# x's first block loaded in two halves over two DMA queues, and idle products moved between its turns

## The chip, the cores and the metric

The kernel runs on one core of a Trainium2 chip. The time is the device time of one execution in microseconds (us); runs of one kernel mostly agree within 0.3%. The engines are TensorE (PE; its weight loads are listed apart as PEld), VectorE (DVE), ScalarE (ACT), GpSimd (POOL) and SyncE (SP), which here only issues DMAs. ScalarE and GpSimd can issue DMAs as well.

## The reference, cut to what matters

One block of a hybrid of attention and mLSTM over 512 tokens of width 1024, float32:

```
h = rms_norm(x, pre_norm_g)                       # x: 512 x 1024
proj = einsum('bsd,dc->bsc', h, w_in)             # 1024 x 4616
aq, ak, av, az, mq, mk, mv, mo, mz, mi, mf = split_columns(proj)
ya = rms_norm(moba_attention(rope(aq), rope(ak), av), attn_out_g) * silu(az)
ym = sigmoid(mo) * norm(mlstm(silu(conv(mq, mk)), mv, mi, mf)) * mlstm_out_g * silu(mz)
x + rms_norm(concat(ya, ym) @ w_out, post_norm_g)
```

Only the very start matters here: x times the columns of w_in that give mv.

## The kernel before, in words

Every large product is made of three products of float32r parts: high by high, high by low, low by high, where a high part is a rounded copy and a low part what is left. x must lie with its features on the partitions, so TensorE turns it first: x is loaded in blocks of 128 features (`X_CHUNKS`, `load_x`, L558 to L561), one block is four tiles of 128 tokens by 128 features, and four products with the identity turn them into a bank of PSUM. ScalarE then copies the bank as the high part (`x_hi`; for block 0 in two halves of 256 tokens, `x_hi_half`, L827 to L831), times the pre-norm weights, and VectorE makes the low part (`x_low`, `x_low_half`, L1124). The norm's factor for each token comes in later.

w_in is cut into slots of 128 rows by 512 columns. SP loads them in order, between the blocks of x: block 0, slot 0, block 1, slot 1 and so on. VectorE rounds slots 0 and 1 (L1128, L1133), ScalarE the later ones (L824), and VectorE makes the low part of each (`cut`, L1101).

The order of work around the change is written out by hand, engine by engine, and each engine runs its own list in order. TensorE's list begins so: six idle products of 512 columns (`keep_busy(6)`, L1568), a turn of the 8 x 128 pre-norm weights (L1574, waits for the identity and their load `par_in`), the turn of tiles 0 and 1 of block 0 and then of tiles 2 and 3 (`turn_x_half(0)` and `turn_x_half(1)`, L1579), four idle products of 256 columns, and then the real products of slot 0 (`mv_slot(0)`, L1606): tiles 0 and 1, tiles 2 and 3 with x's high part, the same with its low part, the turn of block 1 (`turn_x(1)`, L1586), and the four products with the slot's low part. Idle products multiply ones by ones into a bank that is not read. ScalarE's list begins with the load of the pre-norm weights (L853), a small activation that brings its table in (L854), and the two halves of block 0 (L830). `x_squares` (L839) sums the squares of x much later.

Of the kernel before, what the change touches and what calls it, by code (L numbers as in the profile page):

```python
# [23 lines left out]
P = 128  # L24
SEQ = 512
D = 1024
NT = SEQ // P
NK = D // P
AW = 512
# [41 lines left out]
HALF_SEQ = SEQ // 2  # L71
# [10 lines left out]
def width(n):  # L82

    return MZ_W if S_MZ <= n < S_MZ + NK else AW
# [149 lines left out]
def unit(u):  # L234

    return NT - 1 - u // AH, u % AH
# [27 lines left out]
def build(nc, x, pre_g, w_in, i_bias, f_bias, conv_w, conv_b, attn_g, mlstm_g, w_out, post_g, rope, out):  # L264
    with ExitStack() as ctx:
# [3 lines left out]
        def sem(name):  # L269
            return ctx.enter_context(nc.semaphore(name))  # L270
# [54 lines left out]
        def f_part(at, *shape):  # L325
            n = int(np.prod(shape))
            v = farena[:, at:at + n]
            return v if len(shape) == 1 else v.rearrange("p (a b) -> p a b", a=shape[0]) if len(shape) == 2 \
                else v.rearrange("p (a b c) -> p a b c", a=shape[0], b=shape[1])
# [7 lines left out]
        x_sb = f_part(F_X, NT, D)  # L337
# [11 lines left out]
        rows = [gy[0:16, i // 4, i % 4, :] for i in range(8)]  # L349
# [53 lines left out]


        x_in = [sem(f"x_in{c}") for c in range(len(X_CHUNKS))]
        par_in = sem("par_in")
        rope_in = sem("rope_in")
        post_in = sem("post_in")
# [125 lines left out]
        def low_done(eng, n):  # L534

            eng.wait_ge(w_lo_done[n % 2], n // 2 + 1)
# [4 lines left out]
        def turn_tile(n):  # L541

            _, kind, i = TURNS[n]
            return 0 if kind == "ym" else 4, NT - 1 - i


        def store(sp, i):
            t = NT - 1 - i
            for c in range(2):
                cols = slice(c * AW, (c + 1) * AW)  # L550
                sp.wait_ge(out_ready, 2 * i + c + 1)
                sp.dma_start(out[0, t * P:(t + 1) * P, cols], xr[i][:, cols]).then_inc(out_done[i], 16)

        @block.sync
        def _(sp):
            x2 = x.rearrange("b s d -> (b s) d")

            def load_x(c):  # L558
                k, n = X_CHUNKS[c]
                cols = slice(k * P, (k + n) * P)  # L560
                sp.dma_start(x_sb[:, :, cols], x2[:, cols].rearrange("(t p) d -> p t d", p=P)).then_inc(x_in[c], 16)  # L561

            def rows_out(w, m):

                sp.wait_ge(kq_ready, NT * w + m + 1)
                sp.dma_start(kq_dram[w, :, ROT * m:ROT * m + ROT, :], by_dims[:, m, :]).then_inc(kq_out[w], 16)

            def rows_back(w, m):

                sp.wait_ge(kq_out[w], 16 * NT)  # L570
                if w:
                    sp.wait_ge(kt_lo, NT)
                sp.dma_start(whole[:, m, :], kq_dram[w, 2 * m:2 * m + 2].rearrange("h d s -> (h d) s"))\
                    .then_inc(kq_moved[w], 16)

            for n, (mat, kind, k, c) in enumerate(SLOTS):
                if n in X_BEFORE:
                    load_x(X_BEFORE[n])
                if n >= RAW:
                    low_done(sp, n - RAW)  # L580
                w = w_in if mat == "in" else w_out
                if kind == "cols":
                    src = w[0, k * P:(k + 1) * P, c:c + width(n)]
                    dst = w_raw[:, n % RAW, 0:width(n)]
                else:
                    src = w[0, k * P:(k + 4) * P, c:c + MD].rearrange("(k p) c -> p k c", p=P)
                    dst = w_raw[:, n % RAW, :].rearrange("p (k c) -> p k c", k=4)
                sp.dma_start(dst, src).then_inc(raw_in[n % RAW], 16)
                if n == S_QK + 6:
                    sp.wait_ge(ssx_done, NT)  # L590
                    sp.dma_start(gains[:], attn_g.to_broadcast([P, AW])).then_inc(gain_in, 16)
                for w in range(2):
                    for c in range(2):
                        if n == OUT_AT[w] + c:
                            rows_out(w, 2 * c)
                            rows_out(w, 2 * c + 1)
                        if n == BACK_AT[w] + c:
                            rows_back(w, 2 * c)
                            rows_back(w, 2 * c + 1)
                if n == S_AQ + 4:  # L600
                    sp.wait_ge(az_gained, NT)
                    sp.dma_start(gains[:], mlstm_g.to_broadcast([P, AW])).then_inc(gain_in, 16)
            sp.wait_ge(v_lo_done, NT)
            sp.dma_start(post, post_g.to_broadcast([P, D])).then_inc(post_in, 16)

            def load_residual(i):
                t = NT - 1 - i
                sp.dma_start(xr[i], x2[t * P:(t + 1) * P, :]).then_inc(xr_in[i], 16)

            sp.wait_ge(ym_gated, NT)  # L610
            load_residual(0)
            load_residual(1)
            sp.wait_ge(turn_ps, TURN_OF["ym", NT - 1] + 1)
            load_residual(2)
            load_residual(3)
            store(sp, 0)
            store(sp, 1)
            store(sp, 2)
            sp.wait_ge(out_ready, 2 * NT - 1)
            sp.dma_start(out[0, 0:P, 0:AW], xr[NT - 1][:, 0:AW]).then_inc(out_done[NT - 1], 16)  # L620
            sp.wait_ge(out_ready, 2 * NT + 1)
            sp.dma_start(out[0, 0:P, quarter[1]], xr[NT - 1][:, quarter[1]]).then_inc(out_done[NT - 1], 16)
            for i in range(NT):
                sp.wait_ge(out_done[i], 32 + 16 * (i == NT - 1))
# [188 lines left out]
        def _(a):  # L813
# [12 lines left out]
            def x_hi_half(q):  # L826
                half = slice(q * HALF_SEQ, (q + 1) * HALF_SEQ)  # L827
                a.wait_ge(xt_ps, q + 1)
                a.wait_ge(par_done, 1)
                a.activation(xT_hi[:, 0, half], bank[4 + q][:, half], ACT.Copy, scale=pcol[:, R_PRE:R_PRE + 1])\  # L830
                    .then_inc(xt_hi, 1)  # L831
# [7 lines left out]
            def x_squares(t):  # L839
                if t:  # L840
                    a.wait_ge(ssx_done, t)
                for c in range(len(X_CHUNKS)):
                    a.wait_ge(x_in[c], 16)
                a.activation(silu_az[:, 0:2, :].rearrange("p a c -> p (a c)"), x_sb[:, t, :], ACT.Square, accum_out=ssx[:, t:t + 1]).then_inc(ssx_done, 1)
# [6 lines left out]
                             scale=rx[:, t:t + 1]).then_inc(mv_hi_done, 1)  # L851

            a.dma_start(prow[:], pre_g.rearrange("o (c p) -> (o c) p", p=P)).then_inc(par_in, 16)  # L853
            a.activation(ssx[:, 0:1], ones, ACT.Copy)  # L854
            x_hi_half(0)
            x_hi_half(1)
# [2 lines left out]
            for k in range(1, NK):  # L859
                if k > 1:  # L860
                    cut(k)
                    x_hi(k)
                if k >= 5:
                    x_squares(k - 5)
            cut(RING)
            x_squares(NT - 1)
            for n in range(RING + 1, RING + 6):
                cut(n)
# [160 lines left out]
            for s in range(STEPS):  # L1029
# [18 lines left out]
                for kind, what in events:  # L1048
# [7 lines left out]
                    elif kind == "y_sq":  # L1056
                        i, c = what
# [6 lines left out]
                    elif kind == "y_q_sq":  # L1064
                        q = what[0]
# [484 lines left out]
        def _(pe):  # L1550
# [14 lines left out]
            def keep_busy(n, cols=AW):  # L1565

                for _ in range(n):
                    pe.matmul(bank[7][:, 0:cols], ones.to_broadcast([P, P]), ones.to_broadcast([P, cols]), start=True,  # L1568
                              stop=True)
# [4 lines left out]
            pe.transpose(bank[6][:, 0:R_AG], prow[:], ident[0:R_AG, 0:R_AG]).then_inc(par_ps, 1)  # L1574

            def turn_x_half(q):
                pe.wait_ge(x_in[0], 16)
                for t in (2 * q, 2 * q + 1):
                    mm = pe.transpose(bank[4 + q][:, t * P:(t + 1) * P], x_sb[:, t, 0:P], ident[:])  # L1579
                mm.then_inc(xt_ps, 1)  # L1580
# [129 lines left out]


            turn_x_half(0)
            turn_x_half(1)
            keep_busy(4, AW // 2)
            for k in range(NK - 1):
                mv_slot(k)
            mix_slot(0)
# [78 lines left out]
            def turn(n):  # L1796

                _, kind, i = TURNS[n]
                t = NT - 1 - i
                pe.wait_ge(ym_gated if kind == "ym" else ya_gated, i + 1)  # L1800
                if turn_bank(n) == TURN_BANK:
                    pe.wait_ge(masked, min(TURNS[n][0], NU))
                else:
                    pe.wait_ge(ya_summed, (TURNS[n][0] - LAG_YT) // 4 + 1)
                src = ym[:, t] if kind == "ym" else silu_az[:, t]
                for k in range(4):
                    mm = pe.transpose(bank[turn_bank(n)][:, k * P:(k + 1) * P], src[:, k * P:(k + 1) * P], ident[:])  # L1807
                mm.then_inc(turn_ps, 1)
# [90 lines left out]
            for s in range(STEPS):  # L1899
# [16 lines left out]
                if 0 <= u < NU:  # L1916
                    t, h = unit(u)
# [56 lines left out]
```

## Time and profile before

| | us |
|---|---|
| median of 3 runs | 313.82 (313.65 to 314.89) |
| the profiled execution | 313.44 |
| its span, first to last instruction | 311.7 |
| TensorE busy | 305.2 (98%) |
| VectorE, ScalarE, GpSimd busy | 227.4, 164.7, 92.5 |

The profile is of one execution, and its times start with its span. The span is what the engines' instructions cover; the execution's time is 1.74 us more. The busy time of TensorE counts products whose ends are modelled, so it says that TensorE always has work, not how well it is used. The mean granted clock is 0.995.

### The profile page before, as it was taken

The page shows a single profiled execution, that of the slowest core. Times are in us where ns is not written, and L with a number is a line of the kernel's source. Part 1 is how long each engine was busy: PE and PEld are TensorE (multiplying, and loading weights), DVE is VectorE, ACT ScalarE, POOL GpSimd, SP SyncE. Part 2 cuts the span into 40 slices and gives each one's busy share as a digit, 9 for nine tenths or more (in the row PEclk, how much of TensorE's full clock was granted, in tenths as well). Part 3 has the DMA queues.
Part 4 walks back from the last instruction along what each step waited for, and adds up shares of the span by engine and source line. Part 5 has one row for each costly group of instructions (what it writes and reads, how often), then busy time and mean ns, then how long its engine had stood idle before and what let it go on. Part 6 is the DMA issues. An engine that isn't in the chain of part 4 may idle for free.

```text
span 311.7 us, 5015 instructions
## 1 busy us (share of the span) xinstructions
PE 305.2 (98%) x1609; PEld 257.2 (83%) x1609; DVE 227.4 (73%) x511; ACT 164.7 (53%) x338; POOL 92.5 (30%) x110
## 2 busy tenths in 40 slices
PE   8999999999999999999999999999999999999992
PEld 5788888888888888888888899887888888888892
DVE  3544899957999499967999447997676867766534
ACT  3467684578337324384244583494746867452301
POOL 1711005174340004000040017538922984000000
PEclk9999999999999999999999999999999999999997
DMA  7933463565423545752554432410110463310111
GB/s 214 336 79 91 116 196 98 161 199 139 151 67 94 162 142 164 236 167 73 151 173 170 133 103 67 127 63 19 67 67 2 137 219 131 125 67 0 69 67 68
DMA packets 28953, 38.28 MB, mean 123 GB/s; under 512 B 2552, under 2 KB 16236, under 8 KB 28928
## 3 DMA queue, kind: packets, MB, share of 16 engines
q1 hardware_dynamic: 27440, 34.51, 36.7%
q0 software_dynamic: 1328, 3.32, 3.1%
q8 instruction: 13, 0.21, 0.3%
q10 hardware_dynamic: 160, 0.14, 0.1%
q14 instruction: 12, 0.10, 0.1%
HBM read 33.68 MB, written 4.28 MB: 122 GB/s over the span
## 4 chain that ended last, share of the span: by engine, by line
PE 94%; issue 3%; DVE 0%; DVEq 0%; ACT 0%; POOLq 0%; POOL 0%; ACTq 0%
PE bank L1553 25%; PE bank L1555 24%; PE bank L1554 24%; PE bank L1606 4%; PE bank L1924 3%; PE bank L1859 3%; PE bank L1883 3%; PE bank L1701 2%; PE bank L1807 1%; PE bank L1568 1%; PE bank L1586 1%; PE bank L1873 1%; PE bank L1702 1%; PE bank L1895 0%; PE bank L1579 0%
## 5 line engine op out<-in xcount | busy, mean ns | idle before, releaser
L824 ACT ACTIVATE w_hi<-w_raw 128x512 fp32r<-128x512 f32 (+1 forms) x72 | 43.6, 616 | 60.6 <-PE bank L1555 49.4
L1553 PE MATMUL bank<-w_hi,xT_hi 128*128 128x512 f32 (+2 forms) x180 | 71.0, 395 | 0.0
L1555 PE MATMUL bank<-w_hi,xT_lo 128*128 128x512 f32 (+2 forms) x180 | 68.0, 378 | 0.0
L1554 PE MATMUL bank<-w_lo,xT_hi 128*128 128x512 f32 (+2 forms) x180 | 67.7, 376 | 0.0
L1553 PE MATMUL bank<-xT_hi,w_hi 128*128 128x512 f32 x136 | 54.0, 397 | 0.0
L1555 PE MATMUL bank<-xT_hi,w_lo 128*128 128x512 f32 x136 | 53.3, 392 | 0.0
L1554 PE MATMUL bank<-xT_lo,w_hi 128*128 128x512 f32 x136 | 53.1, 390 | 0.0
L1101 DVE TENSOR_TENSOR w_lo<-w_raw,w_hi 128x512 fp32r<-128x512 f32 (+1 forms) x66 | 45.9, 705 | 8.6 <-ACT w_hi L824 8.4
L1555 PEld LDWEIGHTS bank<-w_hi,xT_lo 128*128 128x128 f32 x180 | 33.8, 188 | 5.8
L1553 PEld LDWEIGHTS bank<-w_hi,xT_hi 128*128 128x128 f32 x180 | 33.9, 188 | 5.0 <-issue 0.4
L1554 PEld LDWEIGHTS bank<-w_lo,xT_hi 128*128 128x128 f32 x180 | 34.0, 189 | 4.5
L1555 PEld LDWEIGHTS bank<-xT_hi,w_lo 128*128 128x128 f32 x136 | 25.5, 188 | 5.6
L1554 PEld LDWEIGHTS bank<-xT_lo,w_hi 128*128 128x128 f32 x136 | 25.6, 188 | 4.7
L1553 PEld LDWEIGHTS bank<-xT_hi,w_hi 128*128 128x128 f32 x136 | 25.6, 188 | 4.7
L1027 ACT ACTIVATE rarena<-bank 128x512 fp32r<-128x512 f32 (+3 forms) x32 | 14.0, 437 | 20.8 <-PE bank L1924 20.8
L1419 DVE CUSTOM_DVE_ANT_0 farena<-bank,causal 128x512 f32<-128x512 f32 (+3 forms) x32 | 15.3, 482 | 8.6 <-PE bank L1859 8.2
L1425 DVE TENSOR_TENSOR rarena<-bank,rarena 128x512 fp32r<-128x512 f32 (+3 forms) x32 | 15.6, 486 | 7.8 <-ACT rarena L1027 7.4
L1231 DVE SCALAR_TENSOR_TENSOR farena<-bank,farena 128x512 f32<-128x512 f32 (+3 forms) x16 | 7.8, 490 | 16.4 <-PE bank L1555 16.4
L1019 ACT ACTIVATE farena<-farena,mx 128x512 f32<-128x512 f32 (+3 forms) x32 | 17.9, 560 | 3.4 <-DVE mx L1419 3.3
L1211 DVE SCALAR_TENSOR_TENSOR farena<-farena,pcol 128x512 f32<-128x512 f32 x24 | 18.8, 782 | 0.9
L669 POOL TENSOR_TENSOR vr<-vs,mhalf 128x2 f32<-128x2 f32 x8 | 5.7, 711 | 44.0 <-DVE vs L1270 44.0
L1924 PE MATMUL bank<-ident,farena 128*128 128x128 f32 x80 | 14.6, 280 | 0.0
(214 smaller groups left out, 571.0 us busy)
## 6 DMA issues: line engine op xcount, KB each, us to landing
w_raw<-in_w_in SPq DMA_DIRECT2D x66, 256.0 KB, 2.9
w_raw<-in_w_out SPq DMA_DIRECT2D x16, 256.0 KB, 2.6
farena<-g_rows POOLq DMA_DIRECT2D x4, 640.0 KB, 3.9
kq_rows<-stage SPq DMA_DIRECT2D x8, 256.0 KB
gy<-kq_rows SPq DMA_DIRECT2D x8, 256.0 KB, 3.5
gy<-in_x SPq DMA_DIRECT2D x4, 512.0 KB, 5.2
out_y<-gy SPq DMA_DIRECT2D x7, 256.0 KB, 2.1
w_raw<-in_w_in SPq DMA_DIRECT2D x8, 196.0 KB, 3.4
```

The lines of the kernel that those rows point to most:

```text
L824: a.activation(hi, raw, ACT.Copy).then_inc(w_hi_done, 1)
L1019: a.activation(prob[:, s % 2, 0:n], sm[:, s % 2, 0:n], ACT.Exp, scale=-1.0, bias=mx[:, s:s + 1], accum_out=rsum[:, s:s + 1]).then_inc(prob ...
L1027: a.activation(pT[:, 2 * (u % 2), 0:n], bank[4 + u % 2][:, 0:n], ACT.Copy).then_inc(pt_hi, 1)
L1101: v.tensor_tensor(lo, raw, hi, ALU.subtract).then_inc(w_lo_done[n % 2], 1)
L1211: ins = v.scalar_tensor_tensor(out=acc, in0=u[:, j:j + SEQ], scalar=tap[j], in1=acc, op0=ALU.mult, op1=ALU.add)
L1419: v.tensor_tensor_reduce(sm[:, s % 2, 0:n], bank[score_bank(s)][:, at:at + n], causal[:, SEQ - n:], -Q_SCALE, BIG, ALU.add, ALU.min, mx[:, ...
L1425: v.tensor_tensor(pT[:, 2 * (u % 2) + 1, 0:n], bank[4 + u % 2][:, 0:n], f32(pT[:, 2 * (u % 2), 0:n]), ALU.subtract).then_inc(pt_lo, 1)
L1553: pe.matmul(o, hi, m_hi, start=start, stop=False)
L1554: pe.matmul(o, hi, m_lo, start=False, stop=False)
L1555: return pe.matmul(o, lo, m_hi, start=False, stop=stop)
L1606: mm = pe.matmul(bank[t][:], xs[:, k, t * P:(t + 1) * P], ws, start=k + term == 0, stop=False)
L1924: mm = pe.transpose(bank[4 + u % 2][:, j * P:(j + 1) * P], prob[:, u % 2, j * P:(j + 1) * P], ident[:])
```

## The change

Block 0 of x is loaded by two DMAs in place of one: tokens 0 to 255 by SP as before, at the same place, and tokens 256 to 511 by ScalarE, behind the load of the pre-norm weights, with a semaphore of its own, `x_rest_in`. The turn of tiles 2 and 3 waits for that semaphore in place of `x_in[0]`, and the squares wait for both. Of the four idle products of 256 columns behind the turns, two go between the two halves of the turn.

```
+        x_rest_in = sem("x_rest_in")
...
             def load_x(c):
                 k, n = X_CHUNKS[c]
                 cols = slice(k * P, (k + n) * P)
-                sp.dma_start(x_sb[:, :, cols], x2[:, cols].rearrange("(t p) d -> p t d", p=P)).then_inc(x_in[c], 16)
+                rows = slice(0, SEQ if c else HALF_SEQ)
+                sp.dma_start(x_sb[:, 0:NT if c else NT // 2, cols], x2[rows, cols].rearrange("(t p) d -> p t d", p=P))\
+                    .then_inc(x_in[c], 16)
...
             def x_squares(t):
                 if t:
                     a.wait_ge(ssx_done, t)
+                a.wait_ge(x_rest_in, 16)
...
             a.dma_start(prow[:], pre_g.rearrange("o (c p) -> (o c) p", p=P)).then_inc(par_in, 16)
+            a.dma_start(x_sb[:, NT // 2:NT, 0:P], x.rearrange("b s d -> (b s) d")[HALF_SEQ:SEQ, 0:P]
+                        .rearrange("(t p) d -> p t d", p=P)).then_inc(x_rest_in, 16)
...
             def turn_x_half(q):
-                pe.wait_ge(x_in[0], 16)
+                pe.wait_ge((x_in[0], x_rest_in)[q], 16)
...
             turn_x_half(0)
+            keep_busy(2, AW // 2)
             turn_x_half(1)
-            keep_busy(4, AW // 2)
+            keep_busy(2, AW // 2)
```

## Rows read from the trace of the kernel before

**Rows 1.** The page: busy time with shares, and the last chain by engine.
```profile
PE 305.2 (98%) x1609; PEld 257.2 (83%) x1609; DVE 227.4 (73%) x511; ACT 164.7 (53%) x338; POOL 92.5 (30%) x110
...
PE 94%; issue 3%; DVE 0%; DVEq 0%; ACT 0%; POOLq 0%; POOL 0%; ACTq 0%
```

**Rows 2.** The chain of waits from 0 to 8 us: start, us, what.
```profile
0.85 2.72 PE bank L1568 x6
3.56 0.20 PE bank L1574
3.77 1.04 PE bank L1579 x4
4.81 0.45 PE bank L1568 x4
5.26 1.85 PE bank L1606 x8
```

**Rows 3.** Timeline of TensorE's weight loads, in narrow windows: start, us, what, count.
```profile
3.49 0.18 PEld L1574 LDWEIGHTS bank<-ident,prow 8*128 8x128 f32 x1 [0.84 <-issue]
...
3.69 0.18 PEld L1579 LDWEIGHTS bank<-ident,farena 128*128 128x128 f32 x1
...
3.69 0.29 PEld L1579 LDWEIGHTS bank<-ident,farena 128*128 128x128 f32 x2
...
4.39 0.15 PEld L1568 LDWEIGHTS bank<-const-bfloat16-1.0 128*128 128x128 bf16 x1
...
5.01 0.19 PEld L1606 LDWEIGHTS bank<-w_hi,xT_hi 128*128 128x128 f32 x1
...
5.37 0.19 PEld L1606 LDWEIGHTS bank<-w_hi,xT_hi 128*128 128x128 f32 x1
```

**Rows 4.** Timeline of DMA issues; landings of block 0, slot 0, all x.
```profile
0.81 0.45 SPq L561 DMA_DIRECT2D farena<-in_x  x1
0.81 0.60 ACTq L853 DMA_DIRECT2D prow<-in_pre_norm_g  x1
...
1.32 0.48 SPq L588 DMA_DIRECT2D w_raw<-in_w_in  x1
...
DMA to landing us min/median/max: 2.8/2.8/2.8
...
DMA to landing us min/median/max: 2.9/2.9/2.9
...
DMA to landing us min/median/max: 2.8/5.2/6.8
```

**Rows 5.** Turns of block 0 and of block 1: ns min/median/max, first and last start.
```profile
L1579 PE MATMUL bank<-ident,farena x4: 421/421/474, 3.7 to 4.4; 128*128 128x128 f32 x4
...
L1586 PE MATMUL bank<-ident,farena x4: 270/272/272, 7.0 to 7.3; 128*128 128x128 f32 x4
```

**Rows 6.** Windows: us, busy of PE, PEld, DVE, ACT, POOL, clock, DMA share, GB/s.
```profile
2.00:3.00 1.00, 1.00 (x4) 0.29 (x2) 0.00 (x0) 0.94 (x2) 0.00 (x0) 1.00 0.98 271
...
5.40:9.00 3.60, 3.60 (x19) 2.77 (x18) 2.84 (x6) 1.12 (x2) 0.00 (x0) 1.00 1.02 332
```

**Rows 7.** Timeline of ScalarE and VectorE.
```profile
1.46 1.28 ACT L854 ACT_TABLE_LOAD   x1 [1.46 <-PEq L1966]
...
4.37 0.43 DVE L1128 CAST w_hi<-w_raw 128x512 fp32r<-128x512 f32 x1 [0.40 <-DMA w_raw<-in_w_in]
...
4.42 0.90 ACT L830 ACTIVATE xT_hi<-bank,pcol 128x256 fp32r<-128x256 f32 x2 [1.47 <-PE bank L1579]
...
5.76 0.68 DVE L1101 TENSOR_TENSOR w_lo<-w_raw,w_hi 128x512 fp32r<-128x512 f32 x1
```

**Rows 8.** Timeline of TensorE's products, in narrow windows.
```profile
4.39 0.42 PE L1579 MATMUL bank<-ident,farena 128*128 128x128 f32 x1
...
4.60 0.44 PE L1568 MATMUL bank<-const-bfloat16-1.0 128*128 128x256 bf16 x2
...
5.04 0.70 PE L1606 MATMUL bank<-w_hi,xT_hi 128*128 128x512 f32 x2
```

More of the change, by code:

```diff
@@ L405, in build @@
         x_in = [sem(f"x_in{c}") for c in range(len(X_CHUNKS))]
+        x_rest_in = sem("x_rest_in")
         par_in = sem("par_in")
@@ L560, in load_x @@
                 cols = slice(k * P, (k + n) * P)
-                sp.dma_start(x_sb[:, :, cols], x2[:, cols].rearrange("(t p) d -> p t d", p=P)).then_inc(x_in[c], 16)
+                rows = slice(0, SEQ if c else HALF_SEQ)
+                sp.dma_start(x_sb[:, 0:NT if c else NT // 2, cols], x2[rows, cols].rearrange("(t p) d -> p t d", p=P))\
+                    .then_inc(x_in[c], 16)
             def rows_out(w, m):
@@ L841, in x_squares @@
                     a.wait_ge(ssx_done, t)
+                a.wait_ge(x_rest_in, 16)
                 for c in range(len(X_CHUNKS)):
@@ L853, in _ @@
             a.dma_start(prow[:], pre_g.rearrange("o (c p) -> (o c) p", p=P)).then_inc(par_in, 16)
+            a.dma_start(x_sb[:, NT // 2:NT, 0:P], x.rearrange("b s d -> (b s) d")[HALF_SEQ:SEQ, 0:P]
+                        .rearrange("(t p) d -> p t d", p=P)).then_inc(x_rest_in, 16)
             a.activation(ssx[:, 0:1], ones, ACT.Copy)
@@ L1576, in turn_x_half @@
             def turn_x_half(q):
-                pe.wait_ge(x_in[0], 16)
+                pe.wait_ge((x_in[0], x_rest_in)[q], 16)
                 for t in (2 * q, 2 * q + 1):
@@ L1712, in _ @@
             turn_x_half(0)
+            keep_busy(2, AW // 2)
             turn_x_half(1)
-            keep_busy(4, AW // 2)
+            keep_busy(2, AW // 2)
             for k in range(NK - 1):
```

## The prediction

> **What bounds the kernel now.** I began with the busy row and the engine shares of the chain that ended last [rows 1]. TensorE is busy for 305.2 of 311.7 us and it is 94% of the chain, so the end moves only if TensorE does more or less, or meets a hole. The change touches nothing behind the first weight slot. The profile as a whole is therefore not what decides. What decides is whether the first six microseconds of TensorE have a hole that the change closes, or get one that it opens.
>
> So I read the chain in order of time next, for the first 8 us [rows 2]. It never leaves TensorE. Six idle products run from 0.85, then the product that turns the pre-norm weights, then the four products that turn x's first block, then four idle ones, and real products from 5.26. No DMA and no other engine stands in it. A reader who hopes that an earlier x brings an earlier start must find the wait for x first, and this view shows none.
>
> A chain can hide a short wait, because ends of products are modelled. So I took the timeline of TensorE's weight loads next, which are where its waits sit [rows 3]. The load for the pre-norm product starts at 3.49, and the first load that needs x at 3.69. Between the first and the second load for turning x there is 0.07 us only (3.69 and 3.76: the row of two lasts 0.29, the row of one 0.18, and the second load begins before the first has ended). So a load that waits for nothing may follow so fast. x's block was issued at 0.81 and landed 2.8 us later, at 3.6 [rows 4]. The landing may thus hold back the first turn by up to 3.69 - (3.49 + 0.07) = 0.13 us. By the chain, which gives the pre-norm product the time until 3.77, it holds back nothing. This is all that an earlier first half can win.
>
> The durations also show in which clock this happens. The turning products of x's first block take 421 ns in the median and start over 0.7 us (3.7 to 4.4), those of the second block take 270 to 272 ns and start over 0.3 (7.0 to 7.3), of the same form [rows 5]. By this, the engine is at the lower of its two levels (1.2 GHz) for the turns and at 2.4 GHz in the idle products after them: four of them take 0.45 us of the chain, 0.11 each for 256 columns, while the six before took 0.45 each for 512. The granted clock column says 1.00 from the start, so here durations have to be read and not the column. The rise lies at about 4.7.
>
> **The change part by part.**
>
> *First half on SP's queue.* The load keeps its issue, one instruction of 0.45 us [rows 4], and moves half the bytes. In the microsecond from 2 to 3 the DMA engines are 0.98 busy and move 271 GB/s [rows 6]. 131 KB fewer at this rate is 0.48 us, so the first half lands at about 3.1 in place of 3.6. TensorE's pre-norm product is still in front, at 3.49. The gain at the first turn is between 0 and 0.13 us (above). I take the middle, 0.07. This stretch lies ahead of the clock's rise: what is brought forward there is work at half the rate, and if the rise stays where it is, 0.07 us earlier at 1.2 GHz saves 0.03 us behind the rise.
>
> *The issue on ScalarE's queue.* One more DMA issue, 0.60 us by the one in front of it [rows 4]. Behind it on ScalarE are the table load (1.46, for 1.28 us) and an activation of one column [rows 7]; the table load ends 0.60 later, at 3.34. The next instruction of weight waits until 4.42, so 1.08 us of cover are left, less the small activation, and the cost is 0. Without that cover it would be 0.60. SP's issues keep their number and order.
>
> *The second half's landing, a new wait.* It is issued at 0.81 + 0.60 = 1.41. The first turn of the second half will be the fifth load of TensorE after the pre-norm one, the place that the first idle load has now: 4.39 [rows 3]. Behind this wait in TensorE's queue is everything. From below, it lands as fast as the unloaded rows do, 2.8 and 2.9 us after issue [rows 4]: 4.2 to 4.3, a margin of 0.1 to 0.2 us. It can't be below that in a way that gains, since nothing asks for it before 4.39. From above, the loads on SP's queue take up to 6.8 us to land, median 5.2, but behind up to a megabyte of their own queue [rows 4]. This would be 6.6 to 8.2, a hole of 2.2 to 3.8 us. The nearest rows are the two that were issued in the same first microsecond with little ahead of them, so I take 4.25 and no hole, and keep the rest for the range.
>
> *The first weight slot.* It is issued at 1.32, lands at 4.2 [rows 4], is rounded by VectorE from 4.37 for 0.43 us, to 4.80 [rows 7], and its first reader loads at 5.01 [rows 3]. The sum of x's block and the slot, 512 KB, is the same as before, only the order in which it is served changes. If the second half goes first everywhere the slot lands where it does today; if not, earlier. Neither costs: 0.2 us are in hand.
>
> The Trainium skill speaks against the change here. DMA: Bandwidth & Descriptors, section "Issuing engines are not separate DMA queues", says that transfers started by different engines run on the same 16 DMA engines and interleave, and that issuing from several saves only sequencer time. By that rule the second half brings no bandwidth and only takes turns with the slot; the trace agrees so far that the DMA engines stand at 0.98 and 1.02 busy from 2 to 3 and from 5.4 to 9 us with one queue [rows 6]. The sum by the rule is the same as mine, and a second queue with bandwidth of its own wouldn't lower it either, as TensorE isn't free to use an earlier landing.
>
> *Idle products two and two.* Their number stays four. Two of them move ahead of the rise, and two turns move behind it. A turn takes 0.21 us at the lower level (the three loads from 3.76 to 4.39) and 0.1 at the upper [rows 5]; an idle product of 256 columns takes 0.11 at the upper level (0.45 for four), and 0.22 at the lower, half of one of the six of 512 columns that take 2.72 together [rows 2, 3]. The trade is even, so TensorE's own time stays and the edit costs 0 by itself.
>
> What it does cost is order. ScalarE rounds the two halves of x's first block one after the other, 0.90 us for both from 4.42 [rows 7]. It starts the second at about 4.85, when the fourth turn ends (4.39 + 0.42 = 4.81 [rows 8]). After the change the fourth turn takes the place of the second idle product. That one starts at about 4.77 (the row of two from 4.60 lasts 0.44 and ends at 5.04, and a product at the upper level with 128 columns lasts 0.27 [rows 5, 8]), so the turn ends at 5.04, ScalarE starts 0.04 later at 5.08 and ends at 5.55 with its half of 0.90 and a little. The third real product is the first that reads the second half of x. Its load comes 0.05 after ScalarE's end today (4.85 + 0.47 = 5.32, and 5.37 [rows 3]), so it comes at 5.60. After a load that had to wait, real products go on about 0.1 us later (the load at 5.01 had such a start: the row of two products from 5.04 lasts 0.70, the second of them 0.39 of it, so that one starts at 5.35; at 0.23 a product, 1.85 for eight, the first had its effective start at 5.12 [rows 2, 8]), thus 5.71 in place of the 5.58 where the third product stands now (5.35 + 0.23). This is a hole of 0.13 us, which I take. From below it is 0, if the turn keeps its end at 4.81; from above 0.35, if the two idle products ahead run wholly at the lower level and the turn ends 0.2 later. With the 0.03 of the earlier start it comes to 0.10.
>
> *What follows.* VectorE's two small parts of x start as late as ScalarE's second half, +0.23, so its cut of the first slot starts at 5.99 for 0.68 and ends at 6.67. It is read behind the turn of block 1, whose last product starts at 7.3 [rows 5, 7]: 0.6 us of cover. The sums of squares wait for the new semaphore too, but they wait for all blocks of x already, and the last of these is issued long behind the second half: 0. Everything after that is TensorE's own queue, moved as one block.
>
> **Sum.** 313.44 us for the profiled execution (311.70 span, 1.74 around it), -0.03 + 0.13 = 313.54. The median of the runs is 313.82, 0.38 above the profiled execution; with the same 0.10 it is 313.92, so I say 313.9.
>
> **The rivals.**
>
> *The second half comes too late (slower).* It is on the queue that was issued at 1.41 and takes turns with the slot's packets of 2 KB, with its own of 512 bytes. Place: TensorE's wait ahead of the third turn. It decides from a landing after 4.39. Each 0.1 us is 0.1 us of hole, partly at the lower level. For it: only 0.1 to 0.2 us of margin, engines 0.98 busy. Against it: few bytes ahead of it in its queue (4 KB), and both rows of the first microsecond landed within 2.9. Price: landing at 4.9 gives 0.5 us, 314.4; the far bound of 3.8 gives 317.7.
>
> *The clock rises later (slower).* TensorE has been fed without a hole for 3.9 us from 0.85 when it rises. If a hole ahead of 4.7 puts the rise off, each us at 1.2 GHz loses half a us of work. To be slower by 0.5%, 1.57 us, it would have to come 3.1 us later. For it: one new wait exactly there. Against it: no hole expected, or a short one. Price, for as much again as the first 3.9 us: 1.95 us, 315.8. TensorE: Matmul & The Clock Gate, "The HAM clock gate (the "warmup" mystery)", adds that the moment differs by some 0.5 us either way from run to run; no run here shows that, and by it the time would scatter by 0.25 us.
>
> *The start is taken in full (a little faster).* The load needs x at 3.56, two turns and ScalarE's first half are 0.13 us earlier, and the third product meets no hole because idle products and turns are shorter than modelled: 0.07 to 0.13 us off, 313.7.
>
> *The change doesn't move the landing.* The first half lands with the last packets of whatever shares the engines, still at 3.6. Then only the hole of 0.13 stands: 313.95.
>
> **How the numbers follow.** The forecast, with the last rival in it as nothing can tell them apart, 0.66. A little faster, 0.14. Late second half, 0.15, a third of it beyond 1.5 us. Late clock 0.05, mostly beyond. A measurement tells about 0.5% from no change, that is below 312.2 or above 315.4. Faster than that needs a cause that I don't see: 0.03 for what the views miss. Slower: 0.05 of the late half and 0.03 of the clock, 0.07 in all after rounding down. Same: 0.90. The three runs of before lie between 313.65 and 314.89, so a median moves by some tenths without cause; the range goes from 313.2 (faster case, less 0.5 of scatter) to 314.7 (late half by 0.5, plus 0.3).
>
> **What would show it.** The first load for turning x at 3.56 to 3.70. The third such load at about 4.35 with nothing named as the wait: right; a DMA named, or a start after 4.5: the late half. The third real product at about 5.7, with ScalarE's second half from 5.08. Slot 0's rounding on VectorE at or before 4.4. The same 1.85 us for the eight products after it, plus the hole. Turning products of 270 ns from the fourth on; if those of x's second block still take 421, the clock is late. The forecast is wrong if the first real product starts before 4.9 or after 5.4.

## The result and the profile after

The changed kernel takes 315.22 us (median of 22 runs, 314.20 to 316.98) against 314.30 for the kernel before (22 runs, 313.52 to 316.16). The ratio is 1.0033 with a 95% interval of 1.0019 to 1.0047 (the quotient of the two medians is 1.0029): slower by about 1 us. It is inside the half per cent that I had called no change, but clear of noise, and outside my range of 313.2 to 314.7.

A median says too little here, because the runs fall into two groups with a gap between them. Of the changed kernel's 22 executions 11 lie from 314.2 to 314.8 (the middle one 314.50) and 11 from 315.6 to 317.0 (the middle one 316.25). Of the 22 of before 19 lie below 315.0 (the middle one 314.25) and 3 above 316.0. So the change does two things: it moves the lower group by some 0.3 us (0.25 between its middle runs, 0.37 between its means), and it puts eight more executions of 22 into the upper one, some 1.8 us higher. In means, 0.37 + 8/22 x 1.8 = 1.02, against a measured 0.99 (314.41 to 315.40). The profile after is of an execution of the upper group (316.02 us). The one of before (313.44) is of the lower group and faster than any of its 22 runs, so the two profiles lie 2.58 us apart where the medians lie 0.92 apart: what follows shows where time goes, and not what the change costs on average.

The chain of waits of the changed kernel over the first 30 us, to be held against [rows 2] (start, us, what):

```profile
0.81 0.60 ACTq L857
1.45 4.08 DMA farena<-in_x
5.57 0.69 PE bank L1585 x2
6.26 0.43 PE bank L1574 x2
6.69 2.99 PE bank L1612 x8
9.68 0.44 PE bank L1592 x4
```

A DMA stands in the chain now, where before there was only TensorE: ScalarE's load of x's second half, issued at 1.45, holds everything until 5.57. The real products begin at 6.69 in place of 5.26, 1.43 us later. And the same eight products take 2.99 us in place of 1.85, another 1.14. The sum, 2.57 us, is the whole of the span's growth (311.7 to 314.2, rounded). Behind the turn of block 1 nothing more is lost.

The timeline of TensorE's weight loads shows the place, to be held against [rows 3]:

```profile
3.49 0.18 PEld L1580 LDWEIGHTS bank<-ident,prow 8*128 8x128 f32 x1 [0.84 <-issue]
3.69 0.29 PEld L1585 LDWEIGHTS bank<-ident,farena 128*128 128x128 f32 x2
...
5.57 0.29 PEld L1585 LDWEIGHTS bank<-ident,farena 128*128 128x128 f32 x2 [1.24 <-DMA farena<-in_x]
```

The third turn comes at 5.57, 1.18 us after the 4.39 at which the queue would reach it, and the wait is put down to the DMA. The first turn is at 3.69 as before, although the first half of x landed at 2.9 in place of 3.6: the 0.13 us that I allowed for the start was not there to be won. The landings of the second half and of slot 0, from the rows of their issuing lines:

```profile
DMA to landing us min/median/max: 4.1/4.1/4.1
DMA to landing us min/median/max: 3.9/3.9/3.9
```

4.1 us after 1.45 is 5.5. I had taken 2.8 to 2.9. Slot 0, issued at 1.32 as before, lands at 5.2 in place of 4.2 [rows 4], so it is late as well, but it is no longer what comes last.

That the eight products take longer is the clock. The turns show it, this time with both halves on the low side, to be held against [rows 5]:

```profile
L1585 PE MATMUL bank<-ident,farena x4: 421/448/475, 3.7 to 5.8; 128*128 128x128 f32 x4
...
L1592 PE MATMUL bank<-ident,farena x4: 272/272/273, 9.5 to 9.8; 128*128 128x128 f32 x4
```

The two turns from 5.57 still take what turns take at 1.2 GHz, while before the engine ran at 2.4 GHz from about 4.7. From 9.5 on they take the 272 ns of the upper level. In the eight products between, TensorE goes from one level to the other. At the upper level from the start they would take the 1.85 us of before; wholly at the lower one they take 3.78 ("both halves on SP", below). By the durations of the single products the rise comes at about 9.0.

Windows of the two kernels show what the DMA engines did meanwhile (columns as in [rows 6], where the kernel before has its row from 2 to 3). First the rest of the kernel before, then the changed one:

```profile
3.00:4.40 1.40, 1.40 (x7) 0.88 (x6) 0.20 (x2) 0.00 (x0) 0.00 (x0) 1.00 0.91 280
```

```profile
2.00:3.00 1.00, 1.00 (x4) 0.29 (x2) 0.00 (x0) 1.00 (x1) 0.00 (x0) 1.00 1.00 178
3.00:4.40 1.40, 1.40 (x7) 0.75 (x5) 0.17 (x1) 0.39 (x2) 0.00 (x0) 1.00 0.78 177
4.40:5.60 1.20, 0.43 (x3) 0.03 (x1) 0.29 (x1) 0.47 (x1) 0.00 (x0) 1.00 1.12 354
```

From 2 to 4.4 us they move 178 and 177 GB/s in place of 271 and 280, with the same bytes wanted. They catch up only from 4.4 to 5.6, at 354. The last row has the hole in TensorE too: busy 0.43 of 1.20 us. The same time by queue (packets, MB, share of the 16 engines; q1 is SP's queue, q10 ScalarE's), from 1.7 to 3.0, from 3.0 to 4.4 and from 4.4 to 5.6:

```profile
q1 hardware_dynamic: 299, 0.19, 79.2%
q10 hardware_dynamic: 16, 0.00, 1.3%
...
q1 hardware_dynamic: 118, 0.19, 65.0%
q10 hardware_dynamic: 109, 0.05, 13.0%
...
q1 hardware_dynamic: 540, 0.35, 90.8%
q10 hardware_dynamic: 163, 0.08, 21.6%
```

The 16 packets of q10 in the first stretch are the pre-norm weights. The second half of x, issued at 1.45, is the 272 behind them: none moves before 3.0, 109 up to 4.4, and 163 after that. So it is late in two ways, by a late first packet and by a slow pace. The lower rate from 2 to 3 us belongs to SP's queue by itself, as q10 moves nothing of x then.

### The profile page after: what moved, and what is told of

It reads as the page before. It is cut to its first block, busy times and chain, and to the rows that moved or that the text cites. A ratio compares the mean times of both kernels' runs of the same rounds, so it can differ in the third digit from the quotient of the medians.

```text
span 314.2 us, 5019 instructions
## 1 busy us (share of the span) xinstructions
PE 307.0 (98%) x1609; PEld 258.1 (82%) x1609; DVE 227.1 (72%) x511; ACT 164.5 (52%) x338; POOL 92.5 (29%) x110
## 4 chain that ended last, share of the span: by engine, by line
PE 93%; issue 3%; DMA 1%; DVE 0%; DVEq 0%; ACT 0%; ACTq 0%; POOLq 0%; POOL 0%
PE bank L1559 25%; PE bank L1561 24%; PE bank L1560 24%; PE bank L1612 4%; PE bank L1931 3%; PE bank L1866 3%; PE bank L1890 3%; PE bank L1707 2%; DMA farena<-in_x 1%; PE bank L1814 1%; PE bank L1592 1%; PE bank L1880 1%; PE bank L1708 1%; PE bank L1902 0%; DVEq L265 0%
```

## The experiments

All were compared with runs of the kernel before on the same chip, and each has one profile; a landing in the table is that of this one execution. "Above 315.5" counts the executions of the upper group; in these comparisons the kernel before had 1 of 29, 3 of 31 and 3 of 29.

| kernel | median us | ratio to before, interval | above 315.5 | second half lands, us after its issue |
|---|---|---|---|---|
| the change | 315.22 | 1.0033 (1.0019 to 1.0047) | 11 of 22 | 4.1 |
| only the order | 313.95 | 0.9990 (0.9976 to 1.0004) | 0 of 12 | one load |
| only the load | 315.44 | 1.0047 (1.0025 to 1.0069) | 6 of 12 | 4.0 |
| both halves on SP | 314.95 | 1.0036 (1.0012 to 1.0060) | 4 of 12 | 2.3 |
| slot 0 held | 318.20, one run | | | 2.3 |
| block 1 held | 314.61 | 1.0004 (0.9985 to 1.0023) | 0 of 12 | 3.2 |
| hole filled | 314.71 | 1.0015 (0.9998 to 1.0033) | 0 of 12 | 3.8 |
| hole without a split | 316.98 | 1.0074 (1.0048 to 1.0100) | 7 of 8 | one load |
| issues swapped | 314.11 | 0.9987 (0.9967 to 1.0007) | 0 of 10 | 2.7 |
| issues swapped, again | 314.18 | 0.9992 (0.9975 to 1.0009) | 0 of 12 | 2.7 |
| swapped, four behind | 314.01 | 0.9994 (0.9981 to 1.0008) | 0 of 12 | 2.7 |
| swapped, x turned first | 313.78 | 0.9985 (0.9968 to 1.0002) | 0 of 12 | 2.7 |

### Order or load

The change has two parts, so each was run alone. The order alone is the kernel before with

```
             turn_x_half(0)
+            keep_busy(2, AW // 2)
             turn_x_half(1)
-            keep_busy(4, AW // 2)
+            keep_busy(2, AW // 2)
```

> The kernel before with only the idle products reordered (two between the halves of the turn, two behind); x's first block stays one load. Theory A (the cost of the change is the late second half of x): no wait at the third turn, time within 0.1% of before, ratio 0.999 to 1.001; ScalarE's second half starts at about 5.1 in place of 4.85 and the third real product has a hole of some 0.1 us. Rival B (the order is the cost, through ScalarE's second half and the clock): ratio 1.003 as the whole change had.

The load alone is the changed kernel with the four idle products behind both halves, as in the kernel before.

> The changed kernel with the four idle products behind both halves of the turn, as before; only the load is split over two queues. Theory A: the third turn waits for the second half, which lands at about 5.5; the hole is longer by the two idle products (0.4 us), nothing else differs, so ratio to before 1.003 to 1.005. Rival B: ratio 1.000 to 1.001.

The order costs nothing that can be seen (0.9990, with an interval up to 1.0004), and the load by itself costs what the change does (1.0047, with an interval that holds 1.0033). Rival B fell. The profile of the order alone has a small surprise: its chain is fed, but the first real load waits 0.39 us for the rounding of slot 0, which in this execution landed 3.7 us after its issue and not 2.9, with the same loads as before:

```profile
5.57 0.83 PEld L1606 LDWEIGHTS bank<-w_hi,xT_hi 128*128 128x128 f32 x4 [0.39 <-DVE w_hi L1128]
```

So a landing in this crowd scatters by 0.8 us without any change, and one row of one execution is no price.

The profile of the load alone (314.93 us, lower group) shows the same hole in an execution where the clock was up already:

```profile
3.65 0.20 PEld L1585 LDWEIGHTS bank<-ident,farena 128*128 128x128 f32 x2
5.49 0.20 PEld L1585 LDWEIGHTS bank<-ident,farena 128*128 128x128 f32 x2 [1.64 <-DMA farena<-in_x]
```

```profile
5.93 0.44 PE bank L1574 x4
6.37 1.85 PE bank L1612 x8
```

The first pair are loads, where two take 0.20 us and not the 0.29 of the lower level; the second pair is the chain, with 1.85 for the eight products. The data is as late as in the changed kernel (4.0 us after issue), TensorE stands for 1.64 us, and yet this execution is 1.1 us below the profiled one of the change. The difference lies in the clock: the turn of block 1 starts at 8.22 in place of 9.68, 1.46 us earlier. (0.4 of it is lost again between 240 and 270 us, and so it is in the profile of "issues swapped"; why is open.)

### Which queue, and what is in its way

```
+                if c == 0:
+                    sp.dma_start(x_sb[:, NT // 2:NT, cols], x2[HALF_SEQ:SEQ, cols].rearrange("(t p) d -> p t d", p=P))\
+                        .then_inc(x_rest_in, 16)
```

at the end of `load_x`, with ScalarE's load taken out:

> The changed kernel with the second half issued by SP right behind the first, ahead of slot 0; ScalarE issues only the pre-norm weights. Theory A with the second queue as the culprit: the second half lands by 3.8, slot 0 at 4.5 to 4.8 since its issue is 0.5 us later, no hole at the third turn, ratio to before 0.999 to 1.001. Rival C (splitting itself costs, by two issues and two semaphores, whatever the queue): the second half lands after 4.5 and the ratio is 1.002 or more.

The second half landed 2.3 us after its issue at 1.32, at 3.6, as theory A said, and there was no hole at the third turn. But the ratio was 1.0036: the cost was not saved, it moved. Slot 0 is issued 0.5 us later, at 1.81, and took 4.7 us to land:

```profile
1.81 4.67 DMA w_raw<-in_w_in
...
6.58 0.44 DVE w_hi L1135
...
7.07 3.78 PE bank L1613 x8
10.85 0.85 PE bank L1593 x4
...
14.24 0.43 PE bank L1593 x4
```

This is the chain of that kernel, in its worst execution (318.04 us). The hole is at the first real product now:

```profile
7.06 0.93 PEld L1613 LDWEIGHTS bank<-w_hi,xT_hi 128*128 128x128 f32 x3 [1.88 <-DVE w_hi L1135]
```

With it the clock is late again: the turn of block 1 takes 0.85 us for four at 10.85, where the next takes 0.43 at 14.24. Neither theory had this: I had slot 0 at 4.5 to 4.8. Here the load that is issued behind the two halves pays. That the third load always pays is not shown: with the issues swapped (below) slot 0 is the third large load as well and lands 2.9 to 3.4 us after its issue.

Two kernels took the crowd away. In the first SP holds slot 0 and all behind it until the second half is there:

```
+                if n == 0:
+                    sp.wait_ge(x_rest_in, 16)
```

> The changed kernel with SP's issue of slot 0, and so all behind it, held until the second half of x has landed. It measures the landing on ScalarE's queue with nothing beside it. Theory A1 (it is late because slot 0 and block 1 share the DMA engines or their start with it): it lands 2.8 us or less after its issue, by 4.3. Rival A2 (ScalarE's queue is slow by itself): it lands 4 us after its issue as in the changed kernel, 5.5. The time is worse either way, by 1 to 3 us, as slot 0 is issued at 4.4 or 5.6.

It landed at 3.8, 2.3 us after issue (A1), with 157 of its packets moved between 2 and 3 us, where in the change there were none. ScalarE's queue is as fast as SP's when only the first half of x is beside it. The 1.8 us between 2.3 and 4.1 are made by what SP issues behind that. The time was worse than the 1 to 3 us I expected: 318.20, some 4 us above before, with slot 0's landing at 6.5, a hole of 1.94 us at the first real product, and a clock that rises at about 13.3.

In the second SP holds only block 1 of x, its third issue, and all behind it:

```
+                if n == 1:
+                    sp.wait_ge(x_rest_in, 16)
                 if n in X_BEFORE:
                     load_x(X_BEFORE[n])
```

> The changed kernel with SP's third issue (block 1 of x) and all behind it held until the second half has landed; the second half then shares only with slot 0. If it is block 1, issued in the same two microseconds, that makes the second half late: it lands at 4.3 or earlier and the hole is gone, while block 1 lands at about 6.5, where it is needed at 6.7; ratio 1.000 to 1.003. If it is slot 0: it lands at 5 or later.

3.2 us: between the two. The row of ScalarE's queue from 3.0 to 4.4 us:

```profile
q10 hardware_dynamic: 272, 0.13, 31.5%
```

The first packet is as late as in the change, none before 3.0, but all 272 are through by 4.4. So in these profiles slot 0 beside it goes with the late start, and block 1 with the slow pace. Slot 0 beside it accounts for 0.9 of the 1.8, block 1 and what follows for the other 0.9. Neither of the two outcomes expected came out; both transfers are in the way. Each of these landings is one execution, and equal loads scattered by 0.8 us above, so the split into two equal parts is rough; the ends, 2.3 and 3.8 to 4.1 in three kernels, are not. The hole shrank to 0.36 us by the row below (third turn at 4.69, 0.30 behind its place), and no execution went above 315.5:

```profile
4.69 0.29 PEld L1587 LDWEIGHTS bank<-ident,farena 128*128 128x128 f32 x2 [0.36 <-DMA farena<-in_x]
```

### Is it the hole, or the clock

The same late data, but TensorE fed while it waits:

```
             turn_x_half(0)
-            keep_busy(2, AW // 2)
+            keep_busy(8, AW // 2)
             turn_x_half(1)
```

> The changed kernel with eight in place of two idle products of 256 columns between the halves of the turn. They fill the hole ahead of the late second half (1.2 us: six more of 0.21). The data is as late as in the changed kernel. Theory P (the hole costs twice: once by the late data, once because TensorE stands still and its clock rises later, in about half of the executions): the executions above 315.5 us become rare, the median comes to 314.4, ratio to before 1.001 to 1.002. Rival Q (only the late data costs, the clock does not mind the hole): as the changed kernel, ratio 1.003 to 1.004 with as many executions above 315.5.

```profile
3.76 0.62 PE bank L1585 x2
4.38 1.71 PE bank L1574 x8
6.09 0.43 PE bank L1585 x2
6.51 0.22 PE bank L1574 x2
6.74 2.00 PE bank L1612 x8
```

The real products start at 6.74, no earlier than the 6.69 of the changed kernel, and still the kernel is faster: 314.71 in the median, 0 of 12 executions above 315.5 where the change has 11 of 22. The eight products take 2.00 us and not 2.99. Theory P holds, though the median is 314.71 and not 314.4. Here idle work in a hole buys the clock. By the ratios (1.0015 against 1.0033) the clock is worth about half of the loss, but their intervals overlap, so this share is rough; the counts are not.

The rival way round, a hole with nothing split:

```
                 pe.wait_ge(x_in[0], 16)
+                if q:
+                    pe.wait_ge(x_in[1], 16)
```

> The kernel before, with all of x's first block in one load, the idle products two and two, and the third turn made to wait for block 1 as well, which lands at about 6. A hole of some 1.5 us with no change to any load. If the hole is the price: ratio 1.004 to 1.008 and many executions above 315.5. If the split load does harm in another way than by the hole: ratio 1.000 to 1.002.

Ratio 1.0074, 7 of 8 executions above 315.5. In its profile the third turn waits until block 1 has landed at 6.4, a hole of 2.06 us and not 1.5, and the eight products take 3.04:

```profile
6.52 0.29 PEld L1581 LDWEIGHTS bank<-ident,farena 128*128 128x128 f32 x2 [2.06 <-issue]
```

```profile
6.55 0.66 PE bank L1581 x2
7.21 0.43 PE bank L1568 x2
7.64 3.04 PE bank L1608 x8
```

The bracket names "issue" and no DMA; the chain of the same execution has `DMA farena<-in_x` until 6.42. A hole at this place is enough, with no load changed. Over the kernels the part of executions above 315.5 grows with the hole of the profiled execution, but not strictly: 10 of 111 in the kernel before, none of 36 with the order alone, block 1 held or the hole filled, 17 of 34 with 1.2 to 1.6 us at the third turn, 4 of 12 with 1.9 at the first real product, 7 of 8 with 2.1.

That the upper group is the late clock is read from the profiles. By the durations of single products, the clock rises between 3.5 and 6.8 us in the nine profiled executions of 315.0 us or less, and at about 9.0, 10.1, 13.1 and 13.3 in the four of 316.0 or more. These four all have a hole of 1.2 us or more ahead of the rise. The fifth execution with such a hole, that of the load alone, had its rise at 3.5, ahead of the hole, and stayed below. No execution without a hole was profiled in the upper group, so what puts 10 of 111 executions of the kernel before there is open.

### A version without the hole

If the place in the queue decides, the second half has to be first in its own:

```
-            a.dma_start(prow[:], pre_g.rearrange("o (c p) -> (o c) p", p=P)).then_inc(par_in, 16)
             a.dma_start(x_sb[:, NT // 2:NT, 0:P], x.rearrange("b s d -> (b s) d")[HALF_SEQ:SEQ, 0:P]
                         .rearrange("(t p) d -> p t d", p=P)).then_inc(x_rest_in, 16)
+            a.dma_start(prow[:], pre_g.rearrange("o (c p) -> (o c) p", p=P)).then_inc(par_in, 16)
```

> The changed kernel with ScalarE's two issues swapped: the second half of x first, at 0.81, then the pre-norm weights. If the landing is late because the second half is issued behind slot 0, 0.6 us earlier lets it land before slot 0's bytes, at 3.6 or earlier, with no hole, and the ratio to before is 0.999 to 1.001. If two queues at once are slow whatever the order, it lands at 4.5 or later. The pre-norm weights land by 3.0, in time for 3.49.

It landed at 3.5, 2.7 us after an issue at 0.81, and it takes 2.7 us in the three further profiles with this order, too. Slot 0 and block 1 are issued as in the change. The third turn waits for nothing. The pre-norm weights now land at 3.6, not by 3.0 as I had written, 2.3 us after their issue, and hold the first turn back by 0.25:

```profile
0.81 0.49 ACTq L857
...
1.34 2.30 DMA prow<-in_pre_norm_g
...
3.78 0.24 PE bank L1580
4.02 0.62 PE bank L1585 x2
4.63 0.43 PE bank L1574 x2
5.06 0.43 PE bank L1585 x2
```

The same kernel once more, with more runs:

> The changed kernel with ScalarE's two issues swapped, once more, to narrow the interval. Theory (the order of issue decides the landing, the second half lands by 3.7 and TensorE has no hole): ratio to before 0.998 to 1.000, no execution above 315.5. Rival (the first measurement was lucky): ratio 1.002 or more.

Over both runs 22 executions, none above 315.5; 0.9987 and 0.9992, with 1 in both intervals. 0.6 us earlier at the issue, and a place ahead of slot 0, were worth 2.0 us at the landing.

With the idle products back behind both halves:

```
             turn_x_half(0)
-            keep_busy(2, AW // 2)
             turn_x_half(1)
-            keep_busy(2, AW // 2)
+            keep_busy(4, AW // 2)
```

> The swapped issues, and the four idle products behind both halves of the turn as in the kernel before. With the second half there in time the place of the idle products is worth at most the small wait of the third real product (0.1 us): ratio to before 0.998 to 1.000, the same as with two and two. If the place matters in itself: they differ by 0.5 us or more.

0.9994 against 0.9992: with the data in time the place of the idle products is worth nothing that can be measured.

With the first half of x turned ahead of the pre-norm weights:

```
-            pe.wait_ge(par_in, 16)
-            pe.transpose(bank[6][:, 0:R_AG], prow[:], ident[0:R_AG, 0:R_AG]).then_inc(par_ps, 1)
...
             turn_x_half(0)
+            pe.wait_ge(par_in, 16)
+            pe.transpose(bank[6][:, 0:R_AG], prow[:], ident[0:R_AG, 0:R_AG]).then_inc(par_ps, 1)
             keep_busy(2, AW // 2)
```

> The swapped issues, and TensorE turns the first half of x's block ahead of the pre-norm weights, which land later now (3.6) than the first half of x (3.3). It takes the wait of 0.25 us for the pre-norm weights off the chain, half of which is gained at the lower clock: 0.1 us, ratio to before 0.997 to 1.000. Rival: ScalarE's first half needs the pre-norm column, which now comes later behind the turns, and nothing is gained.

0.9985 (0.9968 to 1.0002), 313.78 us, the lowest median of all, and its interval too holds 1. That it beats the kernel before is not shown. The wait for the pre-norm weights is still there, on their own product now (its load, at 3.99, has 0.33 us ahead of it put down to them), and the first real product stands at 5.66 in its profile. If there is a gain over the kernel before, it is that none of the 46 executions of the four runs with swapped issues went above 315.5, where the kernel before had 3 of 31 and 3 of 29 beside them. If both were alike, all six of these 106 executions would fall on the 60 of before about 3 times in 100, so this is a hint and no more.

## Why the prediction was wrong

*What bounds the kernel* was right: TensorE's own chain, and only its first six microseconds. The chain behind the turn of block 1 moved as one block.

*The first turn*: right in that TensorE was not waiting for x. The first half landed at 2.9 (3.1 forecast), the turn stayed at 3.69, and this was worth 0 rather than 0.03.

*The issue on ScalarE's queue*: right. The table load started at 1.90 instead of 1.46, 0.44 later and not 0.60, and nothing waited for it.

*The second half's landing* is the step that failed. "The nearest rows are the two that were issued in the same first microsecond with little ahead of them, so I take 4.25 and no hole": it landed at 5.5 in the profile, 5.5 and 5.2 in the two other kernels with the same loads. The two rows were not near. They belong to the first and the second large load, and the second half is in time the third, with block 1 0.4 us behind. Slot 0's row carried half a warning, and the row of all x loads the other half: 5.2 in the median, behind others. I put these aside since the bytes ahead were in another queue. With block 1 held, and then slot 0 as well, the time to landing went from 4.1 to 3.2 to 2.3. What is on the DMA engines counts, whatever queue it came by. That is what the Trainium skill says in DMA: Bandwidth & Descriptors, "Issuing engines are not separate DMA queues". I had cited it and used it only to deny a gain. (The order counts as well: with the same loads and the two issues of ScalarE swapped it was 2.7.) Used for a loss, it asks how many bytes are wanted by the time of the landing. As an estimate that would have been block 0 (256 KB), slot 0 (256 KB) and part of block 1, at the 271 GB/s of [rows 6] from 2 us on: 3.9 for the first two, and 4.9 with all of block 1. Block 1 in fact landed only at 6.3, so this counts more ahead of the second half than there was and is still 0.6 us short of 5.5. But it has a hole in it.

*The first weight slot*: wrong too. I had it land at 4.2 or earlier; it landed at 5.2, 5.0 and 4.8 in the three kernels with these loads (4.2, 5.0 and 4.6 in three with the loads of before). In the change it stayed hidden behind the hole, with its rounding done at 5.74, but with the second half in time it would itself have held the first real product: by an estimate, with the 0.05 us that lie between rounding and load in "only the order", its load would come at 5.79 in place of 5.01. With both halves on SP it was the hole.

*The order of the idle products*: I gave the third real product a hole of 0.13. The order alone gave 0.9990, with an interval up to 1.0004, which is 0.13 us: no such cost can be seen, and none of this size excluded.

*The rival "the second half comes too late"* was the right one, with 0.15. Its price, 1 us for each us of hole, gives 1.2 us for the hole of 1.18, near the 0.92 between the medians, but this is luck: the lower group moved by some 0.3 us only, and the rest came by way of the clock, which I had not counted here. In the pair of profiles the same hole goes with 2.57 us. *The rival "the clock rises later"* got 0.05 and came with it in half of the executions, if the upper group is the late clock. I had them as two cases, and a hole can bring both: filled, it left none of 12 in the upper group, and made with no load changed, it put 7 of 8 there. In my own reading the rise (4.7) and the third turn (4.39 [rows 3]) were a few tenths apart, which should have said so. The signs that I had named pointed the right way: a DMA at the third turn, the first real product behind 5.4, and 421 ns in place of 270 for the fourth turn. The one I had named for a late clock, 421 ns at the second block, did not show: block 1's turns took 272, as the rise at about 9.0 came just ahead of them. The upper group lies 1.8 us up, close to the 1.95 I had named.

The clock's rise scatters far more than the sentence I took from the Trainium skill, TensorE: Matmul & The Clock Gate, "The HAM clock gate (the "warmup" mystery)", of half a microsecond either way. In the profiles here it lay ahead of the turn at 3.65 (only the load), near 4.7 (before), near 5.7 (only the order, with no more than the 0.39 us of wait for slot 0), near 6.8 (issues swapped, with 0.25 us of wait), near 9.0 (the change) and near 13.1 (both halves on SP). The measurement decides. My sum took the 4.7 of one profile as fixed. What the engine must do to get its clock was not tried. That holes and late rises go together is shown by filling a hole and by making one.

Open is why the second half's first packet comes only at 3.0 or later with slot 0 beside it, and why the engines moved less then: from 2 to 3 us 178, 206 and 207 GB/s in the three kernels with these loads, against 242 to 271 in the three with the loads of before and 261 to 283 in the four profiles with the issues swapped. From 3.0 to 4.4 us it was 177 in the change and 255 in the kernel with the hole filled, where the second half landed at 5.2, so the rate of that stretch isn't the cause of most of the lateness. Open is also how a hole of 1.2 us costs the lower group only some 0.3 us; no execution of the change from that group was profiled.

## What to carry to other kernels

Do not price a new early transfer by the rows of the first ones; count all that is wanted of the DMA engines by its deadline, on any queue, leave the count a margin (here it came out 0.6 us too early), and issue what TensorE needs first ahead of everything, even of small loads. A hole in TensorE's first microseconds can cost its length, and the clock as well: compare the durations of equal products on both sides of it. Where runs fall into groups, count the groups before explaining the median.

## What the runs showed of the hardware that I had not expected

A load of 128 KB lands 2.3 us after its issue with only 128 KB beside it, issued 0.6 us earlier, and 3.8 to 4.1 us (three profiles) with 256 KB and 256 KB more issued within half a microsecond of it and others behind them. Moved 0.6 us ahead, into the first place of its queue, it takes 2.7 (four profiles). A slot of 256 KB with the same loads around it took 2.9 us in one execution and 3.7 in another. A hole of 1.2 us in TensorE's stream, some 3.5 us after its start, went with 11 of 22 executions some 1.8 us up; filled with six idle products of 256 columns, none of 12 were. The clock's rise, read from durations, lay anywhere from 3.5 to 6.8 us in nine executions with no hole above 0.4 us ahead of it, while the granted clock column read 1.00 in all windows up to 5.6 us.
